# Two transformer blocks on one core: dense projections from three passes over rounded float32 halves to one plain float32 pass, with a nine-slot weight ring

## The reference, cut to what matters

```python
# block 1
z = h @ w_in                      # 2048 x 13360: q, six k/v, gates, lx, ly, ga, gb
o_a = nsa_attention(...)          # compressed + selected + window branches, 16 heads of 128
o_b = gelu(ly) * rg_lru(conv(lx)) # linear recurrence over the 256 tokens
merged = sigmoid(ga) * (o_a @ proj_a) + sigmoid(gb) * (o_b @ proj_b)
x = x + g1 * (merged @ w_out)
x = x + g2 * ((gelu(conv(gate)) * val) @ ffn_down)   # gate, val = h2 @ ffn_up, 6144 each
# block 2
q, k, v, a_gate, u, z, g_a, g_s = split(rms_norm(x) @ w_in_2)
y_a = (attn(q, k, v) * silu(a_gate)) @ w_attn_proj
y_s = (glu(gelu(s5_ssm(u)) @ w_glu + b_glu) * silu(z)) @ w_ssm_proj
x = x + (sigmoid(g_a) * y_a + sigmoid(g_s) * y_s) @ w_out_2
```

## Time and profile before

| | |
|---|---|
| median of 3 runs | 3039.63 us |
| the profiled execution | 3035.36 us |
| its span, first to last instruction | 3033.6 us |
| TensorE busy, matmuls | 2647.2 us, 87% |
| VectorE busy | 1913.4 us, 63% |
| ScalarE busy | 1126.1 us, 37% |
| DMA moved | 548.2 MB, mean 181 GB/s |
| mean granted TensorE clock | 0.932 of 2.4 GHz |

### The profile page before, as it was taken

How to read it: one execution, slowest core, us unless ns; L and a number is a source line. 1 busy time by engine, 2 the same in 40 slices (tenths; PEclk the granted TensorE clock), 3 DMA queues, 4 the chain that set the end, 5 groups by cost and what they waited for, 6 DMA issues and landing times.

```text
span 3033.6 us, 48120 instructions
## 1 busy us (share of the span) xinstructions
PE 2647.2 (87%) x20558; PEld 2570.9 (85%) x20558; DVE 1913.4 (63%) x2538; ACT 1126.1 (37%) x1423; POOL 164.1 (5%) x141
## 2 busy tenths in 40 slices
PE   2499766899999999899999999998898866667899
PEld 2489665899999999899999999998887756666899
DVE  7855444666766565677554555545876687777663
ACT  1122222456533334243443444443444322323332
POOL 0000000000000000000000000000000233332000
PEclk7689888999999999899999999999999978878899
DMA  8765322345677776477555555544543323333454
GB/s 350 279 230 209 129 84 84 125 148 180 235 271 270 280 267 230 156 275 277 197 185 186 183 181 181 183 166 138 177 143 122 119 91 101 104 101 115 153 176 144
DMA packets 237990, 548.20 MB, mean 181 GB/s; under 512 B 10672, under 2 KB 14768, under 8 KB 225360
## 3 DMA queue, kind: packets, MB, share of 16 engines
q1 hardware_dynamic: 233664, 530.31, 50.5%
q0 software_dynamic: 4112, 14.81, 1.4%
HBM read 540.89 MB, written 4.19 MB: 180 GB/s over the span
## 4 chain that ended last, share of the span: by engine, by line
PE 75%; DVE 14%; DVEq 4%; DMA 4%; ACT 2%; issue 2%; PEldq 0%; PEld 0%; ACTq 0%
PE pair L1525 67%; DVE wlo L1074 3%; DMA wraw<-ada_wT_dram 2%; DVE wraw L1051 2%; DMA wraw<-w_in_dram 1%; DVEq L809 1%; PE pair L1531 1%; ACT whi L1069 1%; DVE ssb L812 1%; DVE ssb L810 1%; DVE ssb L815 1%; DVEq L814 1%; PE bank L390 1%; PE bank L566 1%; DVE ssb L808 1%
## 5 line engine op out<-in xcount | busy, mean ns | idle before, releaser
L1074 DVE TENSOR_TENSOR wlo<-wraw,whi 128x1024 fp32r<-128x1024 f32 x809 | 997.7, 1245 | 874.2 <-ACT whi L1069 852.0
L1069 ACT ACTIVATE whi<-wraw 128x1024 fp32r<-128x1024 f32 x809 | 844.5, 1057 | 1632.9 <-PE pair L1525 950.4
L1525 PE MATMUL pair<-h_hi,whi 128*128 128x256 f32 x4128 | 1208.0, 293 | 171.1 <-DVE wlo L1074 90.3
L1525 PE MATMUL pair<-h_lo,whi 128*128 128x256 f32 x4128 | 1192.8, 289 | 0.0
L1525 PE MATMUL pair<-h_hi,wlo 128*128 128x256 f32 x4128 | 1190.6, 288 | 0.0
L1525 PEld LDWEIGHTS pair<-h_hi,whi 128*128 128x128 f32 x4128 | 818.9, 198 | 190.5 <-issue 117.6
L1525 PEld LDWEIGHTS pair<-h_lo,whi 128*128 128x128 f32 x4128 | 819.1, 198 | 0.5
L1525 PEld LDWEIGHTS pair<-h_hi,wlo 128*128 128x128 f32 x4128 | 817.5, 198 | 0.0
L1051 DVE SCALAR_TENSOR_TENSOR wraw<-wraw,cb 128x2048 f32<-128x2048 f32 x96 | 218.7, 2287 | 28.8 <-DMA wraw<-ada_wT_dram 27.7
L1525 PE MATMUL pair<-hid_hi,whi 128*128 128x256 f32 x768 | 218.5, 284 | 0.0
L1525 PE MATMUL pair<-hid_lo,whi 128*128 128x256 f32 x768 | 217.3, 283 | 0.0
(11 more groups left out here) (391 smaller groups left out, 3131.5 us busy)
## 6 DMA issues: line engine op xcount, KB each, us to landing
wraw<-w_in_dram SPq DMA_DIRECT2D x172, 1024.0 KB, 5.2
wraw<-ada_wT_dram SPq DMA_DIRECT2D x96, 1024.0 KB, 5.3
wraw<-ffn_up_dram SPq DMA_DIRECT2D x96, 1024.0 KB, 5.0
wraw<-ffn_down_dram SPq DMA_DIRECT2D x48, 1024.0 KB, 5.0
wraw<-w_out_dram SPq DMA_DIRECT2D x32, 1024.0 KB, 5.1
wraw<-proj_a_dram SPq DMA_DIRECT2D x16, 1024.0 KB, 6.8
wraw<-proj_b_dram SPq DMA_DIRECT2D x16, 1024.0 KB, 6.2
wraw<-w_attn_proj_dram SPq DMA_DIRECT2D x8, 1024.0 KB, 5.0
```

The source lines that it names most:

```text
L1069: sc.activation(whi[:, r, 0:w], wraw[:, z % RAW, 1024 * half:1024 * half + w], ACT.Copy).then_inc(hi_ready, 1)
L1074: ve.tensor_tensor(wlo[:, z % RAW, half, 0:w], wraw[:, z % RAW, 1024 * half:1024 * half + w], whi[:, r, 0:w].bitcast(F32), ALU.subtract).t ...
L1525: ins = te.matmul(pair[:, o, :], w[:, at_w + o * P:at_w + (o + 1) * P], x, start=(k == 0 and o % 2 == 0 and t == 0), stop=(k == last and t ...
```

## The change

Dense matmuls take the raw float32 weights and single float32 activations, one matmul a tile. The weight halves, the activation halves, and the instructions and semaphores that made them are gone; TensorE waits on the slot's load itself. The ring has nine slots. `ada` in the middle of the kernel is done at its own unit, not five units ahead. `res` has its own 16 KB; the store and the two reloads are gone. `m1` is written by the `pa` and `pb` evacuations directly, `sg`, `ob`, `oa`, `at` and `hid` are each written by the operation that computed them; `y_2` lies over `u_2`, and `ph` over `cb`.

```diff
-RAW = 5
-HI = 6
-LEAD = 5
+RAW = 9
...
-    X = {"h1": h1, "m1": m1, "h2": h2, "h3": h3, "m2": m2, "oa": oa, "ob": ob, "hid0": hid, "hid1": hid, "at": at_,
-         "ys": ys, "sg": sg}
+    X = {"h1": h1, "m1": m1, "h2": h2, "h3": h3, "m2": mg2, "oa": oa, "ob": ob, "hid0": hid, "hid1": hid, "at": at_,
+         "ys": y_2, "sg": sg}
...
-    def split(dst, at, n, src):
-        hi, lo = dst
-        ve.tensor_copy(hi[:, at:at + n, :], src)
-        ve.drain()
-        return ve.tensor_tensor(lo[:, at:at + n, :], src, hi[:, at:at + n, :].bitcast(F32), ALU.subtract)
...
         if me == "dve":
-            tt = (t1, t2)[c // 4 % 2]
+            out = dst[:, c:c + 4, :] if shift is None else (t1, t2)[c // 4 % 2]
             for n in range(4):
-                ve.scalar_tensor_tensor(out=tt[:, n, :], in0=res[:, c + n, :], scalar=gain[:, c + n:c + n + 1], in1=r,
-                                        op0=ALU.mult, op1=ALU.mult)
-            ve.drain()
+                ins = ve.scalar_tensor_tensor(out=out[:, n, :], in0=res[:, c + n, :], scalar=gain[:, c + n:c + n + 1], in1=r,
+                                              op0=ALU.mult, op1=ALU.mult)
             if shift is not None:
+                ve.drain()
                 for n in range(4):
-                    ve.tensor_scalar(tt[:, n, :], tt[:, n, :], mod[:, shift + c + n:shift + c + n + 1], None, ALU.add)
-                ve.drain()
-            ins = split(dst, c, 4, tt[:, :, :])
+                    ins = ve.tensor_scalar(dst[:, c + n, :], out[:, n, :], mod[:, shift + c + n:shift + c + n + 1], None, ALU.add)
...
-                ins = split(oa, i * 4 + hd, 1, bank[3][:, 0:1, :])
+                ins = ve.tensor_copy(oa[:, i * 4 + hd, :], bank[3][:, 0, :])
...
-        if me == "dve":
-            j.eng.wait_ge(spilled, 16)
-            ins = ve.drain()
-        yield from j.hand("to_act", "dve", "act", ins)
+        yield from j.hand("to_act", "dve", "act", j.drained())
...
-    def split_act(act, u):
-        (z, half), r, w = unit_slot[u], u % HI, width(u)
-        act.wait_ge(w_loaded[z % RAW], 16 * (z // RAW + 1))
-        if u >= HI:
-            act.wait_ge(pe_units, u - HI + 1)
-        sc.activation(whi[:, r, 0:w], wraw[:, z % RAW, 1024 * half:1024 * half + w], ACT.Copy).then_inc(hi_ready, 1)
-
-    def split_dve(dve, u):
-        (z, half), r, w = unit_slot[u], u % HI, width(u)
-        dve.wait_ge(hi_ready, u + 1)
-        ve.tensor_tensor(wlo[:, z % RAW, half, 0:w], wraw[:, z % RAW, 1024 * half:1024 * half + w],
-                         whi[:, r, 0:w].bitcast(F32), ALU.subtract).then_inc(lo_ready, 1)
-        for z in behind.get(u, ()):
-            ada(dve, z)
...
-            split_unit(j, 2 * b)
-            split_unit(j, 2 * b + 1)
...
-            if i == 3:
-                if me == "dve":
-                    ins = split(m1, 12, 4, rows(res))
-                j.ready["m1"].append(j.give("to_pe", "dve", ins))
-                j.sync("to_pool", "dve", "pool", j.drained())
-                if me == "pool":
-                    po.dma_start(res[:, :, :], xT.rearrange("(c p) t -> p c t", p=P)).then_inc(x_back, 16)
+                ins = ve.tensor_tensor(rows(m1), rows(m1), t2[:, :, :], ALU.add)
+            j.ready["m1"].append(j.give("to_pe", "dve", ins))
...
-        j.sync("to_pool", "dve", "pool", j.drained())
-        if me == "pool":
-            po.dma_start(outT.rearrange("(c p) t -> p c t", p=P), res[:, :, :]).then_inc(spilled, 16)
-
-    def states_done(j):
...
+            j.ready["ys"] = [j.ready["y"]]
...
         def unit(g, gr, u, n):
-            if FIRST <= u + LEAD < N_UNITS:
-                split_dve(dve, u + LEAD)
+            for z in behind.get(u, ()):
+                ada(dve, z)
...
-            pe.wait_ge(lo_ready, u + 1)
-            wh, wl = whi[:, r, :], wlo[:, z % RAW, half, :]
-            terms = lambda k: ((wh, hi[:, k, :]), (wh, lo[:, k, :]), (wl, hi[:, k, :]))
+            if half == 0:
+                pe.wait_ge(w_loaded[z % RAW], 16 * (z // RAW + 1))
+            w = wraw[:, z % RAW, 1024 * half:]
...
                     for o in range(4 if gr.mode == "T" else 2):
-                        for t, (w, x) in enumerate(terms(k)):
-                            ins = te.matmul(pair[:, o, :], w[:, at_w + o * P:at_w + (o + 1) * P], x,
-                                            start=(k == 0 and o % 2 == 0 and t == 0), stop=(k == last and t == 2),
-                                            skip_group_check=True)
+                        ins = te.matmul(pair[:, o, :], w[:, at_w + o * P:at_w + (o + 1) * P], x[:, k, :],
+                                        start=(k == 0 and o % 2 == 0), stop=(k == last), skip_group_check=True)
```

More of the change, by code:

```diff
@@ L110, in put @@
         return nc.alloc_sbuf_tensor_at(name, list(shape), dt, offset=base + at)
-    def put_pair(name, at, n):
-        return put(name + "_hi", at, [P, n, T], F32R), put(name + "_lo", at + n * 1024, [P, n, T], F32R)
     K = 1024
-    z0, z1, z2, rM, rW = 0, 32 * K, 64 * K, 96 * K, 112 * K
-    rWh = rW + RAW * 8 * K
-    rC = rWh + HI * 4 * K
+    zX, rR, rM, rW = 0, 72 * K, 88 * K, 104 * K
+    rC = rW + RAW * 8 * K
     rT = rC + 8 * K
     rS = rT + 8 * K
[L123 to L127, removed]
+    h1, h2, h3 = (put(name, zX, [P, DC, T]) for name in ("h1", "h2", "h3"))
+    oa, ob = put("oa", zX + 16 * K, [P, DC, T]), put("ob", zX + 32 * K, [P, DC, T])
+    m1 = put("m1", zX + 48 * K, [P, DC, T])
+    hid = put("hid", zX + 16 * K, [P, 24, T])
+    res = put("res", rR, [P, DC, T])
     wraw = put("wraw", rW, [P, RAW, 2048])
-    wlo = put("wlo", rW, [P, RAW, 2, 1024], F32R)
-    whi = put("whi", rWh, [P, HI, 1024], F32R)
     cb = put("cb", rC, [P, D])
@@ L133, in build_program @@
     t2 = put("t2", rT + 4 * K, [P, 4, T])
+    z1, z2 = zX + 16 * K, zX + 32 * K
     k2 = put("k2", z2, [P, 2, 4, T])
@@ L156, in build_program @@
     lt = put("lt", rM + 12 * K, [P, 4, T])
[L158 to L170, removed]
+    u_2 = put("u_2", zX + 16 * K, [P, 8, T])
+    y_2 = u_2
+    q_2 = put("q_2", zX + 24 * K, [P, 8, T])
+    ag_2 = put("ag_2", zX + 32 * K, [P, 8, T])
+    mg2 = put("mg2", zX + 24 * K, [P, DC, T])
+    k_2 = put("k_2", zX + 40 * K, [P, 2, T])
+    v_2 = put("v_2", zX + 42 * K, [P, 2, T])
+    z_2 = put("z_2", zX + 44 * K, [P, 8, T])
+    at_ = put("at", zX + 52 * K, [P, 8, T])
+    gs_2 = put("gs_2", zX + 56 * K, [P, DC, T])
+    rs2 = put("rs2", zX + 70 * K, [P, 2, T])
+    sg = put("sg", zX, [P, 8, T])
     kg2 = put("kg2", rM + 9 * K, [P, T])
@@ L639, in lru @@
         if me == "dve":
-            ve.tensor_tensor(lr[:, :, :], lr[:, :, :], t2[:, :, :], ALU.mult)
-            ve.drain()
-            ins = split(ob, i * 4, 4, lr[:, :, :])
+            ve.tensor_tensor(ob[:, 4 * i:4 * i + 4, :], lr[:, :, :], t2[:, :, :], ALU.mult)
         yield
@@ L794, in attention2 @@
                 if me == "dve":
[L795 to L797 removed]
+                    ve.tensor_tensor(at_[:, c:c + 1, :], bank[3][:, 0:1, :], ag_2[:, c:c + 1, :], ALU.mult)
                     ve.drain()
@@ L1190, in evac @@
             if computed("dve"):
-                done(ve.tensor_tensor(rows(res), t1[:, :, :], e[:, :, :], ALU.mult))
+                done(ve.tensor_tensor(rows(m1), t1[:, :, :], e[:, :, :], ALU.mult))
                 ve.drain()
@@ L1284, in evac @@
                 ve.drain()
-                ve.tensor_tensor(rows(mg2), rows(mg2), t2[:, :, :], ALU.add)
+                ins = ve.tensor_tensor(rows(mg2), rows(mg2), t2[:, :, :], ALU.add)
+            j.ready["m2"].append(j.give("to_pe", "dve", ins))
+            if me == "dve":
                 ve.drain()
-                ins = split(m2, 4 * i, 4, rows(mg2))
-            j.ready["m2"].append(j.give("to_pe", "dve", ins))
         elif k == "wout2":
-            if i == 0 and me == "dve":
-                eng.wait_ge(xf_back, 16)
             if computed("dve"):
@@ L1345, in first_out @@
             yield
-        j.sync("to_pool", "dve", "pool", j.drained())
-        if me == "pool":
-            po.dma_start(outT.rearrange("(c p) t -> p c t", p=P), res[:, :, :]).then_inc(spilled, 16)
-    def states_done(j):
-        me, ins = j.me, None
-        if me == "dve":
-            j.eng.wait_ge(*evacuated("gs2", 3))
-        j.sync("to_pool", "dve", "pool", j.drained())
-        if me == "pool":
-            j.eng.wait_ge(S["act_to_dve"], j.ready["y"])
-            po.dma_start(res[:, :, :], outT.rearrange("(c p) t -> p c t", p=P)).then_inc(xf_back, 16)
-        for b in range(2):
-            if me == "dve":
-                ins = split(ys, 4 * b, 4, y_2[:, 4 * b:4 * b + 4, :])
-            j.ready["ys"].append(j.give("to_pe", "dve", ins))
     def before(g, j):
@@ L1399, in build_program @@
         job(lambda j, i=i: lru(j, i), start_of(*a), end_of(*b))
-    job(merged, start_of("pa", 3), end_of("pb", 3))
     job(first_out, start_of("kv2"), start_of("kv2") + 6)
@@ L1468, in _ @@
         prologue(j)
-        def unit(g, gr, u, n):
```

(14 more changed lines are left out.)

58 lines of the change are left out of this document (13 added, 45 removed).

## The result

The changed kernel takes 3215.44 us in the median of four runs (3209.91 to 3218.93) against 3039.84 us, the median of the kernel before with its profiled execution taken in: 1.0576 times, 95% interval 1.0558 to 1.0595. The profiled execution took 3209.9 us, the shortest of the four, and its span is 3208.2 us. The forecast was 3238 us.

A forecast was written before the change was run, and what follows sets the result against it. TensorE was taken to bound the long stage, round trips between engines the first attention and state space model. The stage terms summed to +204 us on 3035.4, giving 3239, rounded down to 3238 us (range 3160 to 3310).

The forecast's parts named there:

- The price of a unit: TensorE's dense work: a unit of eight plain 256-column matmuls takes 3.46 us instead of 2.88 with 24 rounded ones.
- Rival 3: Plain records in a long stream cost less than 0.216 us: about 2370 us, at the page's pace about 2440; 2%.
- Mode N: Matmuls of 512 columns, 134 to 325 us: a unit goes from 2.72 to 3.46 us, 16 units, +12 us.
- Head: 0 to 134 us: nine slots and no splits keep DMA running, last block ends at about 105 us, -28 us.
- To q: 134 to 325 us: T units +20, N +12, gates -5, small matmuls and idle -7, in all +20 us.
- First attention: 325 to 554 us: units +14, weight-slot waits gone -43, halves off the chain -13, clock -7, in all -49 us.
- Long stage: 629 to 2106 us, TensorE-bound: 496 units at 0.58 us more each, +288, idle -2, in all +286 us.
- 2106 to 2409: Three stages after the long one: 72 units +42 less idle given back, forecast as +3, +8 and +8 us.
- State space model: 2409 to 2839 us: rounds fall from 54 to 43 us, only the second wait, 3.6 us, stays: -85 us.
- Rival 1: TensorE's waits stay as long as they are, so longer units hide nothing: +435, 3475 us; 5%.
- Rival 2: The ring does not run ahead, so head and first attention keep 28 + 43 us: 3309 us; 5%.
- Rival 4: TensorE's waits vanish altogether: a floor of some 3095 us, still above 3035; 2%.

The follow-up runs named there:

- price_only: Kernel before with one plain float32 matmul a tile, remainder products left out, splits, waits, five slots and reloads kept: 3437.61 us, 1.1304 of before.
- ring5: Changed kernel with a ring of five slots instead of nine: 3232.86 us, 1.0633 of before.
- lead3: Kernel before with weights split three units ahead of TensorE instead of five, ring of five slots kept: 2972.05 us, 0.9775 of before.
- one_term: Kernel before with one rounded matmul a tile, only the product of the rounded halves, both remainder products left out: 2390.4 us in a single run.

## Why the prediction was right, point by point

*The price of a unit* was forecast as 3.46 us from eight matmuls of another stage and is 3.453 in a stream 136 times as long. The 3.6 rounded matmuls that one plain one costs decide the sign. Rival 3, a cheaper record in a long stream, is refuted by the row of 2176. By the same row the estimate of 2.10 us a unit does not hold that the prediction took from the Trainium skill, TensorE: Matmul & The Clock Gate, section Back-to-back issue gap: a unit took 3.453. (That rival's second figure, 2440 us, does not follow from its own terms: 602 units at 2.10 us with the same -28 and -60 give some 2480. Nothing rests on it.) *Mode N* (+12): 16 x (3.43 - 2.72) = +11. *Gates* (10 us): 8.2.

price_only and ring5 cut the sum into three, by the profiles' spans: price +400.0, relief of VectorE and ScalarE -205.7 (the reloads and the waits of the splits' lead are in it), ring -19.7, together +174.6.

The stages, with the forecast in brackets. "The rest of the busy time" is what TensorE is busy beyond its dense work at the full-clock price (2.88 or 3.453 us a unit), as in the prediction:

- *Head* (-28): -28.5. The cause was right and has two parts: the splits' going gives 11 us (before to ring5), the ring 17.
- *To q* (+20): +10. T and N units cost what was said. For idle time and small matmuls together 7 us were taken off; they shrank by 7 each, and TensorE has no idle time left (201.25 of 201.30).
- *First attention* (-49): -59. **This is the step that failed**, though its number came out near, which is luck. "I count three a round, 14 us, 43 in three rounds. With nine slots the load lies four slots earlier": the waits were there, eight of them and 39 us, but ring5 has four slots fewer and the same stage to 0.1 us, and lead3 removes 38 us with the ring of five and all the splits. The waits belonged to the splits' lead. "sm before L546, 34 us ..., which stays" was wrong for the same reason: what stood ahead of those operations on VectorE was the split that waited for ScalarE that waited for a transfer. It is 6.3 us now. The rest of the busy time fell by 19 us and not 7: the prediction priced the units of this stage at full clock, but on the chain they took 3.48 us each before (19 units) and take 3.61 now (23 units), so that they cost some 3 us more in all and not 14. A round is 56.7 us (170.1 / 3), where 60 was forecast.
- *Long stage* (+286): +279. 496 x 0.573 = +284, less 3 of idle; the rest is rounding.
- *2106 to 2409* (+19): +5. Mis-sized: the rest of the busy time was left as it was, 57 us, and it is 45 now. The idle time fell by 24.5 us where 22 were given back.
- *State space model* (-85): -72. A round is 44.8 us (358.5 / 8) instead of 43. The second wait is as forecast, 29.1 / 8 = 3.6; the first, forecast as none, comes in two rounds, 9.2 us, which is about what was set aside for evacuations. The miss is mostly in the rest of the busy time, 5.3 us a round where 4 were allowed (318.93 - 80 x 3.453 = 42.7 us in all), at a clock of 0.96, not full.
- *End* (+36): +35.

The forecast's sum was 29 us too high. It was 13 too low in the state space model and some 43 too high elsewhere, in the main because the rest of the busy time was taken to shrink by less than it did: outside the head and the state space model it went from 228 to 189 us. The granted clock rose in five of these stages, as the rows show (0.91, 0.84, 0.95, 0.94 and 0.97 before; 0.97, 0.98, 1.00, 1.00 and 1.00 after). That the clock explains all of it was not tested.

Rival 1 (waits stay, 3475 us) is nearest to what price_only did with the splits left in, 3438. Rival 2 supposed a ring that did not run ahead, 3309 us; even five slots cost only 17 us, so this could not have happened. Rival 4's floor, 3095, was not approached.

## What to carry to other kernels

Price an operation by the row of the same operation in the same trace, as a pace in a stream, and multiply by all of it before counting what it relieves: here the relief was real, 206 us, and the price was 400. Use the dear form of a matmul where the preparation of the cheap one stands in a chain between engines, and the cheap one, with its preparation on other engines, where TensorE is the bound. Do not count on a chain to hide the price: the state space model hid two thirds of it, the first attention hardly any. Work done ahead in program order must not ask for data earlier than it can have arrived: a lead that is too long for its ring blocks its engine. Here shortening the lead was one number and worth 67 us; whether a deeper ring would have done the same was not run.

## What the runs showed of the hardware that I had not expected

A rounded matmul of 256 columns starts every 0.120 us in a stream and a plain one leaves two records of 0.2158 us, so three rounded products are 17% cheaper than one plain product, 0.360 against 0.432 us. For 512 columns moving it is 0.227 and 2 x 0.429. And TensorE's price is a price at a clock: in the first attention a unit of three rounded passes took 3.48 us on the chain at a granted clock of 0.84, against 2.88 in the long stage at 0.99. With less work TensorE's clock can fall and take part of the gain back, as in one_term's first attention (0.84 to 0.68).
